# A mixture-of-experts stage: the matrix engine's branch for crowded experts inside the first expert's first piece, and two row gathers ahead of the share arithmetic

## The chip, the cores and the metric

The kernel runs on one core of a Trainium2 chip. The metric is the device time of one execution in microseconds (us): the median of several runs. Engines are named as in the profile: PE is the matrix engine (PEld its weight loads, PEldq its sequencer), DVE the vector engine, ACT the scalar engine, SP the engine that issues the weight transfers (SPq its queue), POOL the general one. A name with a q is the engine's sequencer, which reads the program and hands instructions on.

## The reference, cut to what matters

Two blocks run over the same 256 tokens with 1024 features. The first block has two layers; the second layer ends with a mixture of eight experts, and the change lies there:

```
def moe_swiglu(h, w_router, w_gate, w_up, w_down):
    logits = (xf @ w_router)
    top_logits, top_idx = lax.top_k(logits, TOP_K)          # 2 of 8 experts for a token
    gates = jax.nn.softmax(top_logits, axis=-1)             # the two shares
    ...                                                     # tokens sorted by expert, in blocks of 128
    def expert_block(args):
        xb = xf[tok]
        hb = jax.nn.silu(xb @ w_gate[e]) * (xb @ w_up[e])   # 1024 x 3584 each
        return hb @ w_down[e]                               # 3584 x 1024
    y = yb.reshape(n_rows, D).astype(jnp.float32) * row_gate[:, None]
    out = jnp.zeros((T, D), jnp.float32).at[row_tok].add(y)
```

An expert takes its tokens in blocks of 128. 512 assignments spread over 8 experts, so an expert mostly has fewer than 128; whether one has more is known only when the router has run.

## The kernel before, in words

All products are taken in float32 accuracy from rounded parts: a weight tile is split by ACT into a rounded part (`low_whi`, a CAST) and by DVE into its rest (`low_wlo`, a TENSOR_TENSOR), each in two halves of 128x1024, and PE takes three matmuls of 128x512 for a k-tile of weights: rounded by rounded, rest by rounded, rounded by rest. Weights come in units of 1 MB that SP loads into a ring of buffers as DVE's rests set them free. Each engine's program is written out by hand in one order, and engines meet only at semaphores: `e.wait_ge(*at(...))` waits for the mark that another engine's `then_inc(*mark(...))` sets.

Around the change the work is this. The last projection of the recurrent layer ends (units rg.o.0 to rg.o.3). PE turns the rows and takes the router's logits; DVE picks the two experts of each token, counts, and writes the one-hot selections (`moe_S`). `pe_gather_first` multiplies the normed rows (`moe_hh` and their rest `moe_hl`) by the selections of experts 0 and 1: 32 matmuls of 128x256, into banks 0 to 3, in four parts. ACT scales each part and rounds it (`act_gather`, two ACTIVATEs of 128x256, output `low_hTh`), DVE takes the rest of each part (`dve_gather`, two SCALAR_TENSOR_TENSORs, output `low_hTl`). Then the experts start, as 56 steps (8 experts by 7 pieces of 512 hidden features, `STEPS`); a step has a gate piece (`pe_gate_up` with "g", 24 matmuls into bank 4), an up piece ("u", 24 into bank 5), and from the second step on the down piece of the step before (24). Part q//2 of the gathered rows (mark "xl") is needed by k-tile q of the first gate piece.

Between the gather and the first piece stands `where_over`: each of PE, ACT, DVE and SP loads the largest count of tokens of an expert from memory (TENSOR_LOAD, line 1893), checks it and jumps (COMPARE_BRANCH, line 1894). If the count is over 128, a body follows that computes the tokens beyond the 128th of each expert by plain float32 matmuls; if it isn't, as with these inputs, the engine jumps over the body. PE's body is long: 1872 matmuls. ACT's has 56 ACTIVATEs, DVE's some 300 instructions, SP's 1344 transfers. The body uses banks of the accumulators for its sums.

DVE's order there (`dve_route`): selections, count, the rests of the normed rows, the rests of the unit e0.g0.1 (`lo_after(e, "rg.o.2")`), the share arithmetic (six small operations on `moe_sm`, from `share_e` to `mark("share", 1)`), the four parts of `dve_gather`, the rests of e0.u0.0 (`lo_after(e, "rg.o.3")`), then its own branch.

Of the kernel before, what the change touches and what calls it, by code (L numbers as in the profile page):

```python
# [8 lines left out]
F_DENSE, F_SECOND, F_EXPERT, EXPERTS = 3584, 2816, 3584, 8  # L9
# [33 lines left out]
class Signals:  # L43
# [27 lines left out]
    def at(self, name, *key):  # L71

        if not self.walked and (name, key) not in self.value:
            return self.sem(name), 1
        other, n = self.value[name, key]
        return self.sem(other), n
# [101 lines left out]
def two_block_kernel(nc, A, out):  # L178
    dt, ALU, AX = mybir.dt, mybir.AluOpType, mybir.AxisListType
    AF = mybir.ActivationFunctionType  # L180
# [7 lines left out]
    with ctx:  # L188
        sg = Signals(lambda name: ctx.enter_context(nc.semaphore(name)))
        mark, at, now, also = sg.mark, sg.at, sg.now, sg.also  # L190
# [232 lines left out]
        def lo_after(e, name, half=1):  # L423
            lo_to(e, next_of(name), half)
# [1281 lines left out]
        def dve_route(e):  # L1706
            dve_residual(e, 3, 0, 0)
            dve_residual(e, 3, 0, 1)
            dve_rstd(e, 0)
            dve_hl(e, 0, 0)  # L1710
            dve_hl(e, 0, 1)
            dve_residual(e, 3, 1, 0)
            dve_residual(e, 3, 1, 1)
            dve_rstd(e, 1)

            e.wait_ge(*at("router", "all"))
            e.wait_ge(*at("sum", "logits"))
            e.tensor_copy(mL, AB[0][:, 0:16].rearrange("p (t e) -> p t e", t=2)).then_inc(*mark("logits", "all"))
            e.wait_ge(*at("logits", "all"))
            for tb in range(2):  # L1720
                e.max(mtop[:, tb, :], mL[:, tb, :]).then_inc(*mark("step"))
            e.wait_ge(*now("step"))
            for y in range(2):
                e.tensor_tensor(meq[:, y], mL, by8(mtop[:, :, y]), EQ).then_inc(*mark("step"))
            e.tensor_tensor(mnth[:, 1, :], mtop[:, :, 0], mtop[:, :, 1], EQ).then_inc(*mark("step"))
            e.wait_ge(*now("step"))
            e.tensor_tensor_scan(mcs.rearrange("p k t e -> p (k t e)"), d0[:, :, :, :].rearrange("p k t e -> p (k t e)"),
                                 meq.rearrange("p k t e -> p (k t e)"), 0.0, MUL, ADD).then_inc(*mark("step"))
            e.tensor_scalar(mnth[:, 1, :], mnth[:, 1, :], 1.0, None, ADD).then_inc(*mark("step"))
            e.wait_ge(*now("step"))  # L1730
            for y in range(2):
                e.tensor_tensor(mmask[:, y], mcs[:, y], by8(mnth[:, y]), EQ).then_inc(*mark("step"))
            e.wait_ge(*now("step"))
            e.tensor_tensor(mmask, mmask, meq, MUL).then_inc(*mark("step"))
            e.wait_ge(*now("step"))
            e.tensor_tensor(Mb[:, :, :], mmask[:, 0], mmask[:, 1], ADD).then_inc(*mark("chosen", "all"))
            e.tensor_tensor(mM, mmask[:, 0], mmask[:, 1], ADD).then_inc(*mark("step"))
            e.tensor_tensor(mdiff, mtop[:, :, 1], mtop[:, :, 0], SUB).then_inc(*mark("step"))
            e.wait_ge(*at("rstd", 1))
            e.wait_ge(*now("step"))  # L1740
            e.tensor_tensor(mdiff, rs[:, 1, :, 0], mdiff, MUL).then_inc(*mark("share", 0))
            e.wait_ge(*at("sum", "ranks"))
            e.tensor_copy(posc[:, :], AB[1][:, 0:24]).then_inc(*mark("ranks", "all"))
            also("places", ("all",), "ranks")
            e.wait_ge(*now("step"))
            e.wait_ge(*at("ranks", "all"))
            e.tensor_reduce(mmax, posc[:, 16:24], AX.X, MAX).then_inc(*mark("step"))
            dve_hot(e, 0)
            dve_hot(e, 1)
            e.wait_ge(*now("step"))  # L1750
            e.tensor_copy(cnt[:, :], mmax).then_inc(*mark("count", "all"))
            dve_hl(e, 1, 0)
            dve_hl(e, 1, 1)
            lo_after(e, "rg.o.2")
            e.wait_ge(*at("share_e", "all"))
            e.tensor_scalar(msum, mexp, 1.0, None, ADD).then_inc(*mark("step"))
            e.wait_ge(*now("step"))
            e.reciprocal(mrec, msum).then_inc(*mark("step"))
            e.wait_ge(*now("step"))
            e.tensor_tensor(mg2, mexp, mrec, MUL).then_inc(*mark("step"))  # L1760
            e.tensor_tensor(mt8, mmask[:, 0], by8(mrec), MUL).then_inc(*mark("step"))
            e.wait_ge(*now("step"))
            e.tensor_tensor(mG, mmask[:, 1], by8(mg2), MUL).then_inc(*mark("step"))
            e.wait_ge(*now("step"))
            e.tensor_tensor(mG, mG, mt8, ADD).then_inc(*mark("share", 1))
            for q in range(4):
                dve_gather(e, 0, q)
            lo_after(e, "rg.o.3")


# [39 lines left out]
        def pe_overflow(e):  # L1810
            e.wait_ge(*at("xl", 0, 3))
            for x_ in range(EXPERTS):
                e.wait_ge(*at("ov_hot", x_))
                for tb in range(2):
                    t = e.transpose(bank[7][:, 128 * tb:128 * tb + 128], ov_S[:, tb, :], ident)
                for q in range(KT):
                    for z in range(4):
                        t = e.matmul(bank[q // 4][:, 128 * (q % 4):128 * (q % 4) + 128],
                                     (hh, hl)[z % 2][:, z // 2, 128 * q:128 * q + 128].bitcast(F32), ov_S[:, z // 2, :],
                                     start=z == 0, stop=z == 3)  # L1820
                t.then_inc(*mark("ov_gathered", x_))
                for f in range(7):
                    e.wait_ge(*at("ov_x" if f == 0 else "ov_h", *((x_,) if f == 0 else (x_, f - 1))))
                    for kind, b in (("g", 4), ("u", 5)):
                        for q in range(KT):
                            pe_ov(e, bank[b][:, :], ov_x[:, q, :], (x_, f, kind, q, 0), q == 0, q == KT - 1)
                    e.wait_ge(*at("ov_h", x_, f))
                    for q in range(4):
                        t = e.transpose(bank[6][:, 128 * q:128 * q + 128], ov_h[:, 128 * q:128 * q + 128], ident)
                    t.then_inc(*mark("ov_turned", x_, f))  # L1830
                    e.wait_ge(*at("ov_hT", x_, f))
                    for q in range(4):
                        for n in range(2):
                            pe_ov(e, bank[2 + n][:, :], ov_hT[:, q, :], (x_, f, "d", q, n), (f, q) == (0, 0),
                                  (f, q) == (6, 3))
                e.wait_ge(*at("ov_y", x_))
                for tb in range(2):
                    for n in range(2):
                        t = e.matmul(bank[2 * tb + n][:, :], ov_ST[:, 128 * tb:128 * tb + 128],
                                     ov_y[:, 512 * n:512 * n + 512], start=True, stop=True)  # L1840
                t.then_inc(*mark("ov_scattered", x_))

        def act_overflow(e):
            for x_ in range(EXPERTS):
                for f in range(7):
                    e.wait_ge(*at("ov_used", x_, f, "g", 7, 0))
                    if (x_, f) != (0, 0):
                        e.wait_ge(*at("ov_h", *((x_, f - 1) if f else (x_ - 1, 6))))
                    e.activation(ov_g[:, :], bank[4][:, :], AF.Silu).then_inc(*mark("ov_g", x_, f))

        def dve_overflow(e):
            e.wait_ge(*at("places", "all"))
# [3 lines left out]
            for x_ in range(EXPERTS):  # L1856
# [10 lines left out]
                for f in range(7):  # L1867
                    e.wait_ge(*at("ov_used", x_, f, "u", 7, 0))
                    e.wait_ge(*at("ov_g", x_, f))
                    e.tensor_tensor(ov_h[:, :], ov_g[:, :], bank[5][:, :], MUL).then_inc(*mark("ov_h", x_, f))  # L1870
                    e.wait_ge(*at("ov_turned", x_, f))
                    e.tensor_copy(ov_hT[:, :, :], bank[6][:, :].rearrange("p (k s) -> p k s", k=4)).then_inc(
                        *mark("ov_hT", x_, f))
# [94 lines left out]

        def pe_moe(e):
            pe_route(e)  # L1970
            where_over(e, pe_overflow)
            for c_, (x_, f) in enumerate(STEPS):
                for q in pe_gate_up(e, c_, "g", 0, "msilu"):
                    if c_ == 1 and q == 2:
# [7 lines left out]
                    if x_ % 2 and x_ < EXPERTS - 1 and 2 <= f < 6 and q == 4:  # L1982
                        pe_gather(e, x_ // 2 + 1, f - 2)
                for q in pe_gate_up(e, c_, "u", 1, "mprod"):
                    if x_ and f == 1 and q in (2, 6):
                        pe_scatter(e, x_ - 1, 1, q // 4)
                if c_:
# [1405 lines left out]
```

## Time and profile before

| what | value |
|---|---|
| median of 3 runs | 2329.86 us (2329.62 to 2329.93) |
| the profiled execution | 2329.88 us, its span 2328.1 us |
| PE matmul busy | 2306.1 us (99%), 11387 matmuls |
| DVE busy | 1796.3 us (77%) |
| ACT busy | 1436.0 us (62%) |
| mean granted clock of PE | 0.998 |

The span is the time from the first to the last instruction; some 1.8 us of the execution lie around it. Times in the rows are from the span's start. Matmuls overlap, so that a matmul of 128x512 is shown as 0.39 us while the next starts 0.23 us after it: the pace is read from the starts.

### The profile page before, as it was taken

The page shows a single profiled execution, that of the slowest core. Times are in us where ns is not written, and L with a number is a line of the kernel's source. Part 1 is how long each engine was busy: PE and PEld are TensorE (multiplying, and loading weights), DVE is VectorE, ACT ScalarE, POOL GpSimd, SP SyncE. Part 2 cuts the span into 40 slices and gives each one's busy share as a digit, 9 for nine tenths or more (in the row PEclk, how much of TensorE's full clock was granted, in tenths as well). Part 3 has the DMA queues.
Part 4 walks back from the last instruction along what each step waited for, and adds up shares of the span by engine and source line. Part 5 has one row for each costly group of instructions (what it writes and reads, how often), then busy time and mean ns, then how long its engine had stood idle before and what let it go on. Part 6 is the DMA issues. An engine that isn't in the chain of part 4 may idle for free.

```text
span 2328.1 us, 28882 instructions
## 1 busy us (share of the span) xinstructions
PE 2306.1 (99%) x11387; PEld 1910.2 (82%) x11387; DVE 1796.3 (77%) x2399; ACT 1436.0 (62%) x1985; POOL 7.8 (0%) x17
## 2 busy tenths in 40 slices
PE   9999999899999999999999999999999999999998
PEld 8888889788888888888888888788888877888887
DVE  7755558899999999999899999876754587767554
ACT  6444447677777777777777777554454464555443
POOL 0000000000000000000000000000000000000000
PEclk9999999999999999999999999999999999999999
DMA  8355555599999999999999997545555564555651
GB/s 287 126 197 184 181 181 181 205 343 365 357 358 356 382 349 359 354 380 355 358 361 368 366 353 238 196 144 191 166 195 184 182 209 130 185 185 175 195 182 54
DMA packets 266222, 588.93 MB, mean 253 GB/s; under 512 B 9441, under 2 KB 37361, under 8 KB 265825
## 3 DMA queue, kind: packets, MB, share of 16 engines
q1 hardware_dynamic: 265072, 581.82, 71.4%
q0 software_dynamic: 1008, 5.21, 0.7%
q8 instruction: 91, 1.49, 0.3%
q14 instruction: 51, 0.41, 0.1%
HBM read 585.92 MB, written 1.07 MB: 252 GB/s over the span
## 4 chain that ended last, share of the span: by engine, by line
PE 90%; DVE 8%; ACT 2%; issue 1%; DMA 0%; SPq 0%; DVEq 0%; ACTq 0%
PE ps L106 86%; PE ps L109 4%; DVE low_wlo L121 4%; ACT low_whi L115 1%; DVE s_rot L121 0%; DVE low_nv L127 0%; DVE s_t L121 0%; ACT s_p L112 0%; DVE s_sm L133 0%; DVE ffn_h L121 0%; ACT L112 0%; DMA low_raw<-in_hy_w_in 0%; DVE low_hTl L127 0%; DVE rg_qs L130 0%; ACT low_junk L112 0%
## 5 line engine op out<-in xcount | busy, mean ns | idle before, releaser
L121 DVE TENSOR_TENSOR low_wlo<-low_raw,low_whi 128x1024 fp32r<-128x1024 f32 (+1 forms) x992 | 1158.0, 1212 | 355.7 <-ACT low_whi L115 354.8
L115 ACT CAST low_whi<-low_raw 128x1024 fp32r<-128x1024 f32 (+1 forms) x992 | 984.8, 1043 | 434.9 <-PE ps L106 432.2
L106 PE MATMUL ps<-low_whi,low_hTh 128*128 128x512 f32 (+2 forms) x1616 | 630.1, 393 | 5.3 <-DVE low_wlo L121 3.2
L106 PE MATMUL ps<-low_whi,low_hTl 128*128 128x512 f32 (+2 forms) x1616 | 615.7, 384 | 0.0
L106 PE MATMUL ps<-low_wlo,low_hTh 128*128 128x512 f32 (+2 forms) x1584 | 606.1, 383 | 0.0
L106 PEld LDWEIGHTS ps<-low_whi,low_hTh 128*128 128x128 f32 x1616 | 304.5, 188 | 61.3 <-DVE low_hTl L127 3.6
L106 PEld LDWEIGHTS ps<-low_whi,low_hTl 128*128 128x128 f32 x1616 | 304.1, 188 | 60.3
L106 PEld LDWEIGHTS ps<-low_wlo,low_hTh 128*128 128x128 f32 x1584 | 298.7, 189 | 52.8 <-issue 0.5
L106 PE MATMUL ps<-low_whi,ffn_Th 128*128 128x512 f32 x608 | 243.4, 400 | 0.0
L106 PE MATMUL ps<-low_wlo,ffn_Th 128*128 128x512 f32 x608 | 237.2, 390 | 0.0
L106 PE MATMUL ps<-low_whi,ffn_Tl 128*128 128x512 f32 x608 | 194.3, 390 | 0.0
L106 PE MATMUL ps<-low_whi,moe_xh 128*128 128x512 f32 x448 | 174.7, 390 | 0.0
L106 PE MATMUL ps<-low_whi,moe_xl 128*128 128x512 f32 x448 | 174.3, 389 | 0.0
L106 PE MATMUL ps<-low_wlo,moe_xh 128*128 128x512 f32 x448 | 174.3, 389 | 0.0
L106 PEld LDWEIGHTS ps<-low_whi,ffn_Tl 128*128 128x128 f32 x608 | 114.1, 188 | 25.0
L106 PEld LDWEIGHTS ps<-low_wlo,ffn_Th 128*128 128x128 f32 x608 | 114.4, 188 | 21.8
L106 PEld LDWEIGHTS ps<-low_whi,ffn_Th 128*128 128x128 f32 x608 | 114.3, 188 | 21.7
L121 DVE TENSOR_TENSOR low_wlo<-raw,low_whi 128x1024 fp32r<-128x1024 f32 x102 | 120.1, 1221 | 7.5 <-ACT low_whi L115 7.5
L115 ACT CAST low_whi<-raw 128x1024 fp32r<-128x1024 f32 x102 | 102.0, 1050 | 20.1 <-PE ps L106 20.1
L106 PEld LDWEIGHTS ps<-low_whi,moe_xl 128*128 128x128 f32 x448 | 84.1, 188 | 17.5
L106 PEld LDWEIGHTS ps<-low_whi,moe_xh 128*128 128x128 f32 x448 | 84.1, 188 | 17.2
L106 PEld LDWEIGHTS ps<-low_wlo,moe_xh 128*128 128x128 f32 x448 | 84.1, 188 | 17.2
(359 smaller groups left out, 2315.3 us busy)
## 6 DMA issues: line engine op xcount, KB each, us to landing
low_raw<-in_moe_w_down SPq DMA_DIRECT2D x96, 1024.0 KB, 6.7
low_raw<-in_moe_w_gate SPq DMA_DIRECT2D x95, 1024.0 KB, 6.8
low_raw<-in_moe_w_up SPq DMA_DIRECT2D x94, 1024.0 KB, 6.5
low_raw<-in_w_ffn SPq DMA_DIRECT2D x66, 1024.0 KB, 5.0
low_raw<-in_w_in SPq DMA_DIRECT2D x28, 1024.0 KB, 6.2
low_raw<-in_w_merge SPq DMA_DIRECT2D x24, 1024.0 KB, 5.2
raw<-in_moe_w_up SPq DMA_DIRECT2D x18, 1024.0 KB, 6.8
raw<-in_moe_w_gate SPq DMA_DIRECT2D x17, 1024.0 KB, 6.8
```

What stands on the lines that cost most here:

```text
L106: return self.real.matmul(*a, **k) if self.real else WALK
L109: return self.real.transpose(*a) if self.real else WALK
L115: return self.real.copy(*a) if self.real else WALK
L121: return self.real.tensor_tensor(*a) if self.real else WALK
```

## The change

PE's branch is called inside the first step's up piece, before k-tile 4 of it, in place of ahead of the first gate piece; the other engines' branches stay where they are. Since bank 4 then holds the gate sums and bank 5 the half-made up sums, the body's gate and up sums go to banks 0 and 1, and ACT waits at its body's end until PE has done the body's last scatter. On DVE, parts 0 and 1 of the gathered rows' rests stand ahead of the share arithmetic, parts 2 and 3 behind it.

```diff
@@ dve_route
             lo_after(e, "rg.o.2")
+            dve_gather(e, 0, 0)
+            dve_gather(e, 0, 1)
             e.wait_ge(*at("share_e", "all"))
             e.tensor_scalar(msum, mexp, 1.0, None, ADD).then_inc(*mark("step"))
...
             e.tensor_tensor(mG, mG, mt8, ADD).then_inc(*mark("share", 1))
-            for q in range(4):
-                dve_gather(e, 0, q)
+            dve_gather(e, 0, 2)
+            dve_gather(e, 0, 3)
             lo_after(e, "rg.o.3")
@@ pe_overflow
-                    for kind, b in (("g", 4), ("u", 5)):
+                    for kind, b in (("g", 0), ("u", 1)):
@@ act_overflow
-                    e.activation(ov_g[:, :], bank[4][:, :], AF.Silu).then_inc(*mark("ov_g", x_, f))
+                    e.activation(ov_g[:, :], bank[0][:, :], AF.Silu).then_inc(*mark("ov_g", x_, f))
+            e.wait_ge(*at("ov_scattered", EXPERTS - 1))
@@ dve_overflow
-                    e.tensor_tensor(ov_h[:, :], ov_g[:, :], bank[5][:, :], MUL).then_inc(*mark("ov_h", x_, f))
+                    e.tensor_tensor(ov_h[:, :], ov_g[:, :], bank[1][:, :], MUL).then_inc(*mark("ov_h", x_, f))
@@ pe_moe
             pe_route(e)
-            where_over(e, pe_overflow)
             for c_, (x_, f) in enumerate(STEPS):
...
                 for q in pe_gate_up(e, c_, "u", 1, "mprod"):
+                    if (c_, q) == (0, 4):
+                        where_over(e, pe_overflow)
```

On PE, before, the branch follows the last gather matmul directly (`moe_S`, `moe_hl` are its operands, `moe_cnt` the count):

```order
L106 MATMUL ps<-moe_S,moe_hh 128x256
L106 MATMUL ps<-moe_S,moe_hl 128x256
L1893 TENSOR_LOAD moe_cnt
L1893 ISA x2
L1894 COMPARE_AND_BRANCH
```

and now it stands behind the sixth matmul pair of k-tiles 2 and 3 of the first up piece, whose weights are unit e0.u0.0 (`low_whi_56` rounded, `low_wlo_59` rest):

```order
L106 MATMUL ps<-low_wlo_59,low_hTh 128x512
L106 MATMUL ps<-low_whi_56,low_hTl 128x512
L106 MATMUL ps<-low_whi_56,low_hTh 128x512
L106 MATMUL ps<-low_wlo_59,low_hTh 128x512
L106 MATMUL ps<-low_whi_56,low_hTl 128x512
L1896 TENSOR_LOAD moe_cnt
L1896 ISA x2
L1897 COMPARE_AND_BRANCH
```

36 matmuls moved ahead of the branch: 24 of the gate piece, 12 of the up piece.

On DVE, at the end of the routing, before (`low_hTl` are the rests of the gathered rows, `moe_sm` the share arithmetic, `low_wlo_58` the rests of e0.g0.1, `low_wlo_59` those of e0.u0.0):

```order
L121 TENSOR_TENSOR low_wlo_58<-low_raw_53,low_whi_55 128x1024 x2
L124 TENSOR_SCALAR moe_sm<-moe_sm 128x2
L136 RECIPROCAL moe_sm<-moe_sm 128x2
L121 TENSOR_TENSOR moe_sm<-moe_sm 128x2
L121 TENSOR_TENSOR moe_sm<-moe_sm 128x16 x3
L127 SCALAR_TENSOR_TENSOR low_hTl<-ps,low_col,low_hTh 128x256 x8
L121 TENSOR_TENSOR low_wlo_59<-raw_84,low_whi_56 128x1024 x2
```

and now:

```order
L121 TENSOR_TENSOR low_wlo_58<-low_raw_53,low_whi_55 128x1024 x2
L127 SCALAR_TENSOR_TENSOR low_hTl<-ps,low_col,low_hTh 128x256 x4
L124 TENSOR_SCALAR moe_sm<-moe_sm 128x2
L136 RECIPROCAL moe_sm<-moe_sm 128x2
L121 TENSOR_TENSOR moe_sm<-moe_sm 128x2
L121 TENSOR_TENSOR moe_sm<-moe_sm 128x16 x3
L127 SCALAR_TENSOR_TENSOR low_hTl<-ps,low_col,low_hTh 128x256 x4
L121 TENSOR_TENSOR low_wlo_59<-raw_84,low_whi_56 128x1024 x2
```

Four of the eight operations moved ahead of the six small ones; nothing was added or taken away.

## Rows read from the trace of the kernel before

**Rows 1.** The page: PE's busy line, and the chain that ended last.
```profile
PE 2306.1 (99%) x11387; PEld 1910.2 (82%) x11387; DVE 1796.3 (77%) x2399; ACT 1436.0 (62%) x1985; POOL 7.8 (0%) x17
...
PE 90%; DVE 8%; ACT 2%; issue 1%; DMA 0%; SPq 0%; DVEq 0%; ACTq 0%
```

**Rows 2.** Waits of PE, 440 to 1360 us: total, times, longest.
```profile
PE ps L106 <- DVE low_hTl L127: 2.1, 1, 2.1
PE ps L109 <- DVE ffn_h L121: 0.3, 1, 0.3
```

**Rows 3.** A stretch of experts: length, then PE, PEld, DVE, ACT, POOL, clock, DMA.
```profile
500.00:700.00 200.00, 199.77 (x919) 165.36 (x918) 182.65 (x177) 153.11 (x173) 0.00 (x0) 1.00 0.97 353
```

**Rows 4.** PE in order of time: start, duration, operation, idle before it.
```profile
442.40 0.28 PE L106 MATMUL ps<-moe_S,moe_hl 128*128 128x256 f32 x1
444.73 0.47 PE L106 MATMUL ps<-low_whi,low_hTh 128*128 128x512 f32 x1 [2.05 <-DVE low_hTl L127]
...
451.89 0.39 PE L106 MATMUL ps<-low_whi,low_hTh 128*128 128x512 f32 x1
...
454.61 0.39 PE L106 MATMUL ps<-low_whi,low_hTh 128*128 128x512 f32 x1
```

**Rows 5.** Lines 1893 and 1894: durations in ns, then the start in us.
```profile
L1893 PEldq TENSOR_LOAD <-moe_cnt x1: 490/490/490, 440.4 to 440.4; - x1
...
L1894 PEldq COMPARE_BRANCH  x1: 3320/3320/3320, 441.2 to 441.2; - x1
L1894 ACTq COMPARE_BRANCH  x1: 45/45/45, 443.5 to 443.5; - x1
L1894 DVEq COMPARE_BRANCH  x1: 72/72/72, 445.3 to 445.3; - x1
L1894 SPq COMPARE_BRANCH  x1: 55/55/55, 449.9 to 449.9; - x1
```

**Rows 6.** The chain of waits, 443 to 445 us: start, duration, what.
```profile
443.17 0.80 DVE low_hTl L127 x2
443.97 0.76 issue
```

**Rows 7.** DVE in order of time.
```profile
439.84 2.35 DVE L121 TENSOR_TENSOR low_wlo<-low_raw,low_whi 128x1024 fp32r<-128x1024 f32 x2
442.11 0.17 DVE L124 TENSOR_SCALAR moe_sm<-moe_sm 128x2 f32<-128x2 f32 x1
...
443.09 0.87 DVE L127 SCALAR_TENSOR_TENSOR low_hTl<-ps,low_col,low_hTh 128x256 fp32r<-128x256 f32 x2
...
446.23 2.35 DVE L121 TENSOR_TENSOR low_wlo<-raw,low_whi 128x1024 fp32r<-128x1024 f32 x2
450.47 2.36 DVE L121 TENSOR_TENSOR low_wlo<-raw,low_whi 128x1024 fp32r<-128x1024 f32 x2 [1.89 <-ACT low_whi L115]
```

**Rows 8.** ACT in order of time: parts 0 and 1 of the gathered rows.
```profile
441.28 0.84 ACT L112 ACTIVATE low_hTh<-ps,low_col 128x256 fp32r<-128x256 f32 x2 [1.30 <-PE ps L106]
...
442.00 0.84 ACT L112 ACTIVATE low_hTh<-ps,low_col 128x256 fp32r<-128x256 f32 x2
```

**Rows 9.** Instruction transfers: 442.1 to 443.2, 446.4 to 447.7, 457.3 to 458.4 us.
```profile
q8 instruction: 1, 0.02, 5.2%
...
q8 instruction: 1, 0.02, 5.0%
...
q8 instruction: 1, 0.02, 5.3%
```

**Rows 10.** SP's transfers, 449 to 456 us.
```profile
454.80 0.39 SPq L145 DMA_DIRECT2D raw<-in_moe_w_up  x1
```

**Rows 11.** PE after the pause at 414 us; two stretches with the clock ahead of the last two columns.
```profile
416.28 0.50 PE L106 MATMUL ps<-low_whi,rg_yh 128*128 128x512 f32 x1 [2.16 <-DVE low_wlo L121]
...
415.00:419.00 4.00, 2.34 (x9) 1.61 (x9) 3.94 (x17) 3.88 (x5) 0.00 (x0) 1.00 1.05 394
...
445.70:449.10 3.40, 3.40 (x9) 2.65 (x8) 2.87 (x4) 0.12 (x1) 0.00 (x0) 0.50 0.32 117
```

## The prediction, made before the changed kernel ran

> **What bounds the kernel now.** I read the page first: PE is busy for 99% of the span and makes up 90% of the chain that ended last [rows 1]. So the time moves only by what moves PE's own row of matmuls, and I looked for every place in the expert stage where PE stands. The waits of PE from the gather to the end of the experts are two: 2.1 us once, put down to DVE's gathered rows, and 0.3 us once [rows 2]. In a 200 us stretch of experts PE is busy for 199.77, at full clock, DVE for 182.65 and ACT for 153.11 [rows 3]: PE sets the pace there, and a microsecond that PE starts earlier is a microsecond that it ends earlier. That holds to the end only as PE's work is a chain; nothing in the second block runs by a clock of its own.
>
> Then PE in order of time [rows 4]. The last gather matmul starts at 442.40, the first gate matmul at 444.73: 2.05 us idle. From 451.89 to 454.61 twelve matmuls of 128x512 start, 0.227 us apart. From 444.73 to 454.61 there are 36 of them (24 of the gate piece, 12 of the up piece); at that pace they would take 8.16 us, and they took 9.88, so 1.72 us were lost. The reason stands in [rows 11]: from 445.7 to 449.1 the granted clock was 0.50, the lower of its two levels (1.2 GHz). It fell about a microsecond after the pause. So the place holds two losses: the pause and, behind it, the slow clock.
>
> The profile names DVE as the cause of the pause. The chain says more [rows 6]: DVE's part 0 ends at 443.97, and then 0.76 us pass as "issue" before PE moves. [rows 5] say what they are: PE's sequencer loads the count at 440.4, starts its COMPARE_BRANCH at 441.2, and that takes 3320 ns, so it ends at 444.56, 0.17 us before the first gate matmul. On ACT, DVE and SP the same line takes 45 to 72 ns. PE's rows were late at 443.97, but the branch was later. During it the queue that brings instructions moved a block [rows 9]: PE's body is so long that the place it jumps to had to be brought. SP, with a body of 1344 transfers, shows a short branch at 449.9, yet its next transfer is issued at 454.80 [rows 10], while the rests that free its buffer (those of e0.u0.1) ended at 450.47 + 2.36 = 452.83 [rows 7]: there too about 2 us are gone behind a long jump.
>
> The Trainium skill, "Runtime: NRT & Kernel Launch", section Instruction fetch mechanics, states that a taken branch to code outside the fetched window forces a fetch of the target's page before execution goes on. By that rule the cost travels with the branch, and the trace agrees (3320 ns and one block moved). The skill's "Advanced Engine Details and Errata", section Control Flow Timing, puts a compare-and-branch at about 108 ns; taken by itself that would make the moved branch free, which is the first rival below.
>
> **The change, part by part.**
>
> Start of the gate piece. Two things held it: the branch (444.56) and part 0 of the rests (443.97). The branch is gone from here. On DVE the rests of e0.g0.1 end at 439.84 + 2.35 = 442.19 [rows 7]; ACT's part 0 is done at 441.28 + 0.84 = 442.12 [rows 8], so DVE starts part 0 at about 442.18, and its two operations take 0.87 [rows 7]: 443.05. PE follows in about 0.08, at 443.13. Gain against 444.73: 1.60 us. Part 1 (ACT 442.84, [rows 8]) is done at about 443.85, and k-tile 2 wants it at 443.13 + 6 x 0.227 = 444.49. Then the share arithmetic, 443.09 - 442.11 = 0.98 us [rows 7], stands between; part 2 ends at about 443.85 + 0.98 + 0.79 = 445.6, and k-tile 4 wants it at 443.13 + 2.72 = 445.85; part 3 at 446.4 against 447.2. Part 2 is the tight one, with 0.2 us. The DVE total is unchanged, so the rests of e0.u0.0 end at 448.6 to 448.7 as they do now (446.23 + 2.35 = 448.58), and the first k-tiles of the up piece, due at 443.13 + 24 x 0.227 = 448.58, find their first half long done (447.4).
>
> The slow clock. The pause ahead of the gate piece shrinks from 2.05 us to about 443.13 - 442.68 = 0.45 us. That is less than a quarter of the one behind which the clock fell, and close to the 0.3 us of [rows 2], behind which no pace was lost. I take the 1.72 us as given back.
>
> The new place of the branch. PE's sequencer must have passed the wait of k-tile 2 of the up piece before it gets to the count: that is the end of e0.u0.0's rests, 448.6 to 448.7. It hands on twelve matmuls and loads the count at about 448.85 (0.2 us later; in the trace 0.46 us passed between the last wait ahead of it, DVE's `moe_hl`, and the load, so 0.1 to 0.5 is the range). From load to first matmul it took 444.73 - 440.4 = 4.33 us [rows 4, 5]. So the next matmul starts at about 453.2. Meanwhile PE has what was handed on: 36 matmuls from 443.13 last until 443.13 + 8.16 = 451.29. New pause: 453.2 - 451.29 = 1.91 us. The branch is hidden behind twelve matmuls (2.7 us) and no more, since the rests of e0.u0.0 come only as the up piece starts. Bounds: 0, if the jump costs on PE what it shows on the other engines; 2.3 with the late load and a block that comes 0.1 slower beside weight transfers. I take 1.91, nearest to the one PE row.
>
> Behind it: queued behind the branch are PE's k-tiles 4 to 7, whose rests (e0.u0.1) end by 452.83 even without any shift [rows 7], and everything of PE after. ACT waits for PE's release of the weight buffers and shifts with it; SP and POOL are passed by no moved instruction. The other banks, the changed operands and ACT's added wait lie in bodies that are jumped over: nothing. In exchange the share is made 1.65 us later, and it is needed only at the first scatter in the second expert.
>
> Sum at the 37th matmul: before it starts at 454.61, after at 453.2: -1.60 - 1.72 + 1.91 = -1.41 us. On the profiled execution's 2329.88 (0.02 above the median) that gives 2328.47, say 2328.5 us.
>
> **The rivals.**
>
> The moved branch costs PE nothing, for a short or prefetched jump. For it: 45 to 72 ns on three engines [rows 5]. Against: SP's late transfer, and PE's own row. Then PE goes on at 451.3: -3.3 us, 2326.6.
>
> The clock falls again, in or behind the new pause. This is the one on the other side. In the trace, a pause of 2.05 us was followed by the lower level for 3.4 us, while one of 2.16 us, just ahead of 416.28, was not (415 to 419 shows 1.00, [rows 11]). The new one of 1.9 us is a little shorter than either, but of their kind; before it PE has run 36 matmuls without a stop, where before the fall it had run the smaller matmuls of the gather. If it falls, 1.72 us come back: -1.41 + 1.72 = +0.31, 2330.2, slower than before. It decides from a pause of about 2 us on.
>
> A second block of instructions is late. Behind the branch as it was, the next block moved between 446.4 and 447.7 the second of [rows 9], that is 1.9 to 3.1 us after the branch ended; with the 1.4 us that lay between the first block's transfer and the branch's end, it may be there only 4.5 us after the branch. The new landing place is 36 matmuls further on in the same code, so that much nearer to the block's end. If fewer than some 20 matmuls (4.5 us) stand between, PE pauses once more, by up to 3.1 us with six left; the middle is 1.6: +0.2, 2330.1, and at worst 2331.6. For it: after 444.7 the third block moved only between 457.3 and 458.4 the third of [rows 9], when PE was 48 matmuls past the old landing; if that marks the block's end, it lies 50 or more matmuls behind it, so some 14 to 25 behind the new one. That is at the edge; I think it mostly covered.
>
> The gain is eaten later, by DVE or ACT, and the time stays at 2329.9. Against: rows 2, no wait of PE on a weight rest in the whole stage.
>
> **How the numbers follow.** Forecast 0.52, free branch 0.12, the clock falls again 0.18, second block late 0.12, eaten 0.06. All of them lie between -3.3 and +1.8 us. 0.2% is 4.7 us, about what a measurement of this kernel can tell from no change; the pause and the slow clock together are 3.8 us, so even their whole loss would not reach it. Faster by over 0.2%: 0.02. Slower: 0.03, for two of the rivals at once with a worse size. Within: 0.95. The range goes from the free branch to the second block with 0.2 us of the measurement: 2326.5 to 2330.5. The likeliest case's own range is 2328.0 to 2328.9.
>
> **What would show it.** First gate matmul at 443.1 to 443.2, with some 0.4 us idle before it; full clock from 442 to 451; PE's TENSOR_LOAD at about 448.9 and a COMPARE_BRANCH of about 3.3 us; a pause of 1.7 to 2.1 us inside the up piece, ended by no other engine, its next matmul near 453.2; no lower clock behind it; the same distance of 1.4 us at the end of the experts. It is wrong if PE's branch is short, if the sequencer loads the count well before the up piece starts, if the clock falls, or if part 2 of the rests comes after k-tile 4 is due.

## The result, and the profile after

The change costs 4.6 us. Over 16 runs of each kernel on the same chip the median is 2334.52 us after (2332.03 to 2336.56) against 2329.89 before (2327.64 to 2331.37): a ratio of 1.0019 [1.0012, 1.0026], slower, though by just under the 0.2% that counted as a change in the forecast. The forecast was 2328.5 us, and all 16 runs lie above its range. The execution with the profile took 2333.81 us, its span 2332.0 us, 3.9 us more than before. In these 16 runs the mean granted clock goes with the time: 0.998 in the one of 2332.03 us, 0.995 in the one of 2336.56 us.

The page first: PE's busy line and the chain, which answer to [rows 1], and the group of matmuls with most idle time before it.

```profile
PE 2308.6 (99%) x11387; PEld 1912.2 (82%) x11387; DVE 1795.8 (77%) x2399; ACT 1436.2 (62%) x1985; POOL 7.8 (0%) x17
...
PE 90%; DVE 7%; ACT 2%; issue 1%; DMA 0%; SPq 0%; DVEq 0%; ACTq 0%
...
L106 PE MATMUL ps<-low_whi,low_hTh 128*128 128x512 f32 (+2 forms) x1616 | 630.8, 393 | 7.6 <-issue 4.1
```

PE has as many matmuls and is busy 2.5 us longer, for which the clock further down is the only cause that the rows show; and one group now shows 4.1 us of idle time that no engine ended. The waits of PE from the gather to the end of the experts (total, times, longest) say the same against [rows 2]: the pause of 2.1 us on DVE is 0.4 us, the one of 0.3 us is gone, and one of 4.1 us is new.

```profile
PE ps L106 <- issue: 4.1, 1, 4.1
PE ps L106 <- DVE low_hTl L127: 0.4, 1, 0.4
```

PE in order of time after the change (start, duration, operation, idle before it), to be laid beside [rows 4]:

```profile
442.69 0.28 PE L106 MATMUL ps<-moe_S,moe_hl 128*128 128x256 f32 x1
443.38 0.50 PE L106 MATMUL ps<-low_whi,low_hTh 128*128 128x512 f32 x1 [0.41 <-DVE low_hTl L127]
...
451.44 0.39 PE L106 MATMUL ps<-low_whi,low_hTl 128*128 128x512 f32 x1
455.96 0.79 PE L106 MATMUL ps<-low_whi,low_hTh 128*128 128x512 f32 x1 [4.13 <-issue]
456.55 0.63 PE L106 MATMUL ps<-low_wlo,low_hTh 128*128 128x512 f32 x1
456.98 0.63 PE L106 MATMUL ps<-low_whi,low_hTl 128*128 128x512 f32 x1
...
462.94 0.60 PE L109 MATMUL ps<-low_cst,ffn_h 128*128 128x128 f32 x4
```

The gate piece starts 1.35 us earlier (443.38 against 444.73), although the gather itself ended 0.29 us later in this execution. 36 matmuls run at 0.23 us apart; then PE stands for 4.13 us, and the matmuls behind are 0.43 us apart. The 37th matmul starts at 455.96, 1.35 us later than before; the transposes of `ffn_h`, which come 18 matmuls later (twelve that end the up piece and six of the next gate piece), start at 462.94, where before they did at 458.70: 4.24 us later. Nearly all of that is kept to the end (3.9 us).

The count's load and the branch in the changed kernel (durations in ns, then the start in us; [rows 5] of before):

```profile
L1896 PEldq TENSOR_LOAD <-moe_cnt x1: 485/485/485, 449.0 to 449.0; - x1
...
L1897 ACTq COMPARE_BRANCH  x1: 45/45/45, 443.8 to 443.8; - x1
L1897 DVEq COMPARE_BRANCH  x1: 72/72/72, 445.8 to 445.8; - x1
L1897 PEldq COMPARE_BRANCH  x1: 6068/6068/6068, 449.8 to 449.8; - x1
L1897 SPq COMPARE_BRANCH  x1: 55/55/55, 450.2 to 450.2; - x1
```

PE's branch jumps over a body of the same instructions, for the same count, and takes 6.07 us where it took 3.32. The next rows say what is different around it: SP's transfers, then the packets of three windows by queue (count, MB, share of the engines), from the branch's start to 453.4, from there to 454.5, and around 460. The last row is of the kernel before, the first 0.9 us of its branch (441.2 to 442.1).

```profile
448.94 0.37 SPq L145 DMA_DIRECT2D raw<-in_moe_w_gate  x1
455.06 0.94 SPq L145 DMA_DIRECT2D raw<-in_moe_w_up  x2
```

```profile
q1 hardware_dynamic: 513, 1.03, 90.8%
q14 instruction: 2, 0.02, 1.6%
...
q8 instruction: 1, 0.02, 5.8%
q1 hardware_dynamic: 15, 0.01, 3.8%
...
q1 hardware_dynamic: 240, 0.46, 100.8%
q8 instruction: 1, 0.02, 5.2%
```

```profile
DMA packets 0, 0.00 MB, mean 0 GB/s; under 512 B 0, under 2 KB 0, under 8 KB 0
```

SP issues 1 MB of weights 0.9 us before PE's branch. While these packets run, no block of PE's instructions moves. It starts at 453.45, as the weights run dry, 3.62 us after the branch began; before the change it started 0.94 us after (442.18 against 441.24), when no weight transfer was under way: SP's was issued at 442.22. The rest is as it was: 1.03 us for the block (0.91 before), 1.42 us from there to the branch's end (1.47 before).

The clock ahead of the last two columns, in three stretches (length, PE, PEld, DVE, ACT, POOL, clock, DMA): the 36 matmuls, the stretch of low clock behind the pause, and one ahead of the place of the change.

```profile
443.30:451.80 8.50, 8.43 (x36) 6.68 (x36) 7.99 (x18) 7.28 (x11) 0.00 (x0) 1.00 0.58 176
434.60:438.00 3.40, 3.40 (x21) 3.33 (x20) 2.47 (x20) 3.37 (x6) 0.00 (x0) 0.50 0.01 2
...
455.10:461.90 6.80, 5.94 (x14) 4.68 (x15) 0.42 (x1) 0.36 (x1) 0.00 (x0) 0.50 0.84 297
```

The lower level (1.2 GHz) begins in the pause, 0.9 us before PE goes on, and lasts 6.8 us, twice as long as in [rows 11]. The 18 matmuls from there to the transposes took 462.94 - 455.96 = 6.98 us, where before it took 458.70 - 454.61 = 4.09: 2.89 us for the clock.

Last DVE, whose rests the share arithmetic now interrupts:

```profile
444.41 0.66 DVE L121 TENSOR_TENSOR moe_sm<-moe_sm 128x2 f32<-128x2 f32 x4
445.00 1.65 DVE L127 SCALAR_TENSOR_TENSOR low_hTl<-ps,low_col,low_hTh 128x256 fp32r<-128x256 f32 x4
446.57 2.35 DVE L121 TENSOR_TENSOR low_wlo<-raw,low_whi 128x1024 fp32r<-128x1024 f32 x2
449.29 4.63 DVE L121 TENSOR_TENSOR low_wlo<-raw,low_whi 128x1024 fp32r<-128x1024 f32 x4 [0.38 <-issue]
461.48 0.69 DVE L121 TENSOR_TENSOR ffn_h<-ffn_g,ps 128x512 f32<-128x512 f32 x1 [7.56 <-PE ps L106]
```

The rests of e0.u0.0 end at 446.57 + 2.35 = 448.92, PE loads the count at once (448.98), and later DVE waits 7.56 us for PE: DVE holds nothing up.

### The profile page after: what moved, and what is told of

It reads as the page before. It is cut to its first block, busy times and chain, and to the rows that moved or that the text cites. A ratio compares the mean times of both kernels' runs of the same rounds, so it can differ in the third digit from the quotient of the medians.

```text
span 2332.0 us, 28882 instructions
## 1 busy us (share of the span) xinstructions
PE 2308.6 (99%) x11387; PEld 1912.2 (82%) x11387; DVE 1795.8 (77%) x2399; ACT 1436.2 (62%) x1985; POOL 7.8 (0%) x17
## 4 chain that ended last, share of the span: by engine, by line
PE 90%; DVE 7%; ACT 2%; issue 1%; DMA 0%; SPq 0%; DVEq 0%; ACTq 0%
PE ps L106 86%; PE ps L109 4%; DVE low_wlo L121 3%; DVE s_rot L121 0%; ACT low_whi L115 0%; DMA low_raw<-in_hy_w_in 0%; DVE s_t L121 0%; DVE low_hTl L127 0%; ACT s_p L112 0%; DVE s_sm L133 0%; DVE low_nv L127 0%; ACT L112 0%; DVE rg_qs L130 0%; DVE ffn_h L121 0%; ACT ffn_g L112 0%
## 5 line engine op out<-in xcount | busy, mean ns | idle before, releaser
L115 ACT CAST low_whi<-low_raw 128x1024 fp32r<-128x1024 f32 (+1 forms) x992 | 984.9, 1043 | 442.2 <-PE ps L106 439.3
```

Source lines behind the costliest of these rows:

```text
L115: return self.real.copy(*a) if self.real else WALK
```

## The experiments

Theory A, formed on these rows: the block of code at the branch's target waits for the transfers that are already on their way, so the branch costs 3.3 us in a quiet spot and more beside a weight transfer; the lower clock comes with the long pause. Against it stood: a branch that is dearer at this place whatever the transfers do (B, the landing place); and DVE's new order, which may hold PE up (C). "Fetch" below is the start of the 16 KB block on queue 8 after the branch's start, as the packets of the trace have it. Before, in the three sessions: 2331.05, 2329.98 and 2329.87 us (medians of 33, 27 and 15 runs). The ratios with their 95% intervals are those on record; they are not the quotients of these medians, and some differ from them by up to 0.06%.

**No weight transfer under way.** SP takes its own branch one transfer earlier, and then holds that transfer until PE is past the up piece.

```diff
-            sync_weights(e, 4, routed)
+            sync_weights(e, 4, routed - 1)
             where_over(e, sync_overflow)
-            sync_weights(e, routed, len(units))
+            e.wait_ge(*at("sum", "u", 0))
+            sync_weights(e, routed - 1, len(units))
```

> The changed kernel, with SP's branch one transfer earlier and the one weight transfer of 1 MB that was in flight during PE's branch (issued at 448.9 us) held until PE has made the first up sums. In the changed kernel PE's COMPARE_BRANCH took 6.07 us in place of the 3.32 us at its old place; its block of code began to move only 3.6 us after the branch began, as that transfer ended, and before it was 0.9 us. Theory A, the block waits behind the weight transfer: the branch takes 3.2 to 3.6 us here, the pause shrinks from 4.1 to about 1.5 us, and the time falls by 2.7 us and by what the clock gives back, to 2328.5 to 2331. Theory B, the landing place in the code or the crossing of a block just before the branch makes it long: 6 us, pause 4 us, time within 1 us of the changed kernel's 2334.5.

PE's branch, then PE behind it, then the packets from 452.2 to 453.5 and from there to 454.6:

```profile
L1897 PEldq COMPARE_BRANCH  x1: 3708/3708/3708, 452.2 to 452.2; - x1
```

```profile
455.94 0.50 PE L106 MATMUL ps<-low_whi,low_hTh 128*128 128x512 f32 x1 [1.76 <-DVE low_wlo L121]
```

```profile
DMA packets 0, 0.00 MB, mean 0 GB/s; under 512 B 0, under 2 KB 0, under 8 KB 0
...
q8 instruction: 1, 0.02, 5.3%
```

The fetch comes 1.36 us after the branch, alone on the engines; the branch takes 3.71 us, a little more than the 3.6 expected, the pause is 1.76 us (1.91 was forecast for the change), and no lower clock follows. 2329.76 us, a ratio to before of 0.9998 [0.9989, 1.0007]. The slowdown is gone with the transfer. A gain isn't shown, and the interval doesn't exclude the 1.4 us of the forecast.

**Half the weight transfer.** After, with 512 KB of the 1 MB issued ahead of SP's branch and the rest held.

```diff
-            sync_weights(e, 4, routed)
+            sync_weights(e, 4, routed - 1)
...
+            load(e, "half", u.raw[:, 0:2, :], u.src[:, 0:2, :])
             where_over(e, sync_overflow)
+            e.wait_ge(*at("sum", "u", 0))
+            e.wait_ge(*at("d_half", "in"))
+            e.dma_start(u.raw[:, 2:4, :], u.src[:, 2:4, :]).then_inc(sg.sem(f"raw{u.slot.i}"), 16)
```

> The changed kernel with only the first half (512 KB) of the weight transfer issued at 448.9 us; the second half is held until PE has made the first up sums. The block of PE's code began to move 3.6 us after the branch began beside the whole transfer (1 MB) and 1.4 us after it with none in flight. Theory A, the block waits until the transfer in flight is through: the start comes in between, 2 to 2.8 us after the branch began, and the branch takes 4.3 to 5.1 us. Rival, any transfer in flight costs the same (a slot in a queue, not the bytes ahead): 3.3 us or more to the start, branch 5.7 us or more.

PE's branch, and the packets of its first 2.4 us:

```profile
L1897 PEldq COMPARE_BRANCH  x1: 4808/4808/4808, 449.2 to 449.2; - x1
```

```profile
q1 hardware_dynamic: 271, 0.52, 76.5%
q14 instruction: 1, 0.01, 0.8%
```

Fetch 2.43 us after the branch, pause 2.87 us, one execution at 2331.03 us. Between no transfer (3.71 us) and 1 MB (6.07), as A has it. SP's own branch is one more thing beside PE's: in the changed kernel it comes 0.4 us after it (450.21). Here it comes just as near (449.55 against 449.18) and PE's is 1.3 us shorter, so it isn't SP's jump that makes the difference.

**The same cost put into the kernel before.** Before, with 768 KB more of weights issued by SP just ahead of PE's branch. They go to a tile that nothing reads; ACT and DVE wait for them behind their own branches (two lines that the diff leaves out).

```diff
-            sync_weights(e, 4, routed)
+            sync_weights(e, 4, routed - 2)
+            e.wait_ge(*at("hl", 1, 1))
+            load(e, "extra", extra[:, :, :], rows_of(A["moe_w_gate"][0, 0], 0, 384, 0, 512))
+            sync_weights(e, routed - 2, routed)
```

> The kernel before, in its old order, with one more transfer of 768 KB by SP (weights into a region that is free then; nobody reads them), issued when DVE has the last rests of the normed rows, at about 440.0 us, a microsecond ahead of PE's branch at 441.2. Theory A: the block of PE's code starts only as that transfer ends, 2.5 to 4 us after the branch began in place of 0.9, the branch takes 5 to 6.5 us in place of 3.3, the first gate matmul comes at 446.5 to 448 and the time rises by 2 to 3 us. Theory B (landing place): the branch stays at 3.3 us and the time at that of before within 0.5 us.

The transfer and the branch, and PE behind it:

```profile
439.50 0.37 SPq L145 DMA_DIRECT2D ov_extra<-in_moe_w_gate  x1
```

```profile
L1895 PEldq COMPARE_BRANCH  x1: 5200/5200/5200, 440.8 to 440.8; - x1
```

```profile
446.16 0.77 PE L106 MATMUL ps<-low_whi,low_hTh 128*128 128x512 f32 x1 [3.93 <-DVE low_hTl L127]
```

With the branch at its old place and the old order of PE's and DVE's work, the transfer alone makes it 5.20 us (fetch after 2.73), the pause 3.93 us and the clock low for 6.8 us, from 0.8 us before PE goes on. The first gate matmul comes at 446.16, just before the 446.5 to 448 expected. 2332.53 us, 1.0013 [1.0004, 1.0022]. That speaks against B and C. The packets of the 1.1 us from the block's start also show what it waits for:

```profile
q1 hardware_dynamic: 147, 0.29, 86.6%
q8 instruction: 1, 0.02, 5.4%
```

Another 0.29 MB of weights moved beside it; SP had issued its next transfer at 441.77, after the branch. It looks as if only what was ahead of the block had to pass first. The kernels with a short body below agree: SP issues another 1 MB 1.4 us after PE's branch began (452.99 with three pieces), and the fetch starts 3.5 to 3.7 us after the branch, as in the changed kernel (3.62).

**No branch.** After, with PE's branch and body left out.

```diff
-                        where_over(e, pe_overflow)
+                        if e.real is None:
+                            pe_overflow(e)
```

> The changed kernel without PE's branch and its body (left out: PE's part of the work for experts with over 128 tokens, which these inputs never need); the other engines keep theirs. If the branch is the whole cause (theories A and B alike), there is no pause in the first up piece, no lower clock behind it, and the time is 4.1 us of pause and 2 to 3.4 us of slow clock below the changed kernel's 2334.5, that is 2326.5 to 2328.5: 1.5 to 3.5 below the kernel before. If something else in the change slows it (the order on DVE, the second block of code), the time stays above 2330.

No pause stands in its place, and the transposes start at 456.06 (458.70 before). 2327.93 us, 0.9993 [0.9984, 1.0002]. The whole branch is worth 1.6 us by this ratio (0.0007 x 2330), which the interval can't tell from nothing; its other end is 3.7 us, so how much the best place could bring stays open.

**One half of the change at a time.** First only PE's branch moved, with DVE's old order; then only DVE's new order, in the kernel before.

```diff
-            dve_gather(e, 0, 0)
-            dve_gather(e, 0, 1)
             e.wait_ge(*at("share_e", "all"))
...
-            dve_gather(e, 0, 2)
-            dve_gather(e, 0, 3)
+            for q in range(4):
+                dve_gather(e, 0, q)
```

> Only PE's branch is moved, with its banks; DVE's order is that of before. The gate piece then starts when part 0 of the rests is there, at about 444.0 (after 0.98 us of share arithmetic) in place of 443.1 to 443.4, and everything up to the branch's load hangs on DVE's rests of e0.u0.0, which do not move. So the branch lies at the same time, 6 us long under theory A and B, the pause before it is 1 us longer and the one at the branch 1 us shorter: the same time as the changed kernel within 1 us, 2333.5 to 2335.5. If the DVE order mattered by itself, it would differ by more.

```profile
PE ps L106 <- issue: 2.9, 1, 2.9
PE ps L106 <- DVE low_hTl L127: 1.3, 1, 1.3
PE ps L109 <- DVE ffn_h L121: 0.3, 1, 0.3
```

The waits of PE with the branch alone moved: 1.3 us for the gathered rows instead of 0.4, so DVE's order does bring its 0.9 us there, and 2.9 us at the branch, which takes 5.74 us (fetch after 3.32). 2332.08 us, 1.0010 [1.0001, 1.0019]. The new place of the branch is enough for a slowdown, though one at the edge of what these runs can tell. It was expected at 2333.5 to 2335.5 and came out below. Both halves together reach the 37th matmul no sooner (13.27 us after the last gather matmul, 13.00 here), since the end of PE's branch hangs on DVE's rests of e0.u0.0; what DVE's new order adds is a longer pause there, 4.1 us in place of 2.9, and this profile shows no lower clock with the shorter one. The runs fit that: the mean granted clock is 0.998 in seven of the 11 here, and in three of the 16 of the changed kernel.

```diff
+            dve_gather(e, 0, 0)
+            dve_gather(e, 0, 1)
             e.wait_ge(*at("share_e", "all"))
...
-            for q in range(4):
-                dve_gather(e, 0, q)
+            dve_gather(e, 0, 2)
+            dve_gather(e, 0, 3)
```

> The kernel before with the new order on DVE alone. PE's branch ends at 444.5 whatever DVE does, so the gate piece starts at 444.7 as before: 2329.9 within 0.5 us, and the branch 3.3 us long. If the rests of the gathered rows had held PE (as the profile's releaser says), the start would come 0.7 to 1.5 us earlier.

DVE's order alone: pause 2.09 us instead of 2.05, branch 3.36 us, 2329.8 us, 1.0000 [0.9991, 1.0009]. The branch ended last there, so earlier rows bring nothing. The profiled execution shows no lower clock behind this pause and took 2327.60 us, the fastest of its 11; one came behind the same pause in [rows 11], in an execution of 2329.88. The medians are the same: which execution shows it is not fixed by the kernel.

**A shorter body, so a shorter jump.** After, with a body of one expert; then with one expert and 1, 3 or 5 of its 7 pieces. The jump passes 234, 66, 122 and 178 matmuls instead of all experts' (some 476, 134, 248 and 362 instructions of PE, an estimate from the code with a weight load for each matmul).

```diff
-        ov_all = [p for x_ in range(EXPERTS) for p in ov_pieces(x_)]
+        ov_all = [p for x_ in range(1) for p in ov_pieces(x_)]
...
-            for f in range(7):
+            for f in range(1):
                 for kind, w in (("g", A["moe_w_gate"]), ("u", A["moe_w_up"])):
```

> The changed kernel with a short body on all four engines: only the first expert's part (234 matmuls on PE in place of 1872; the parts of experts 1 to 7 are left out, which these inputs never run). Place of the branch, transfers in flight and matmul order are those of the changed kernel. Theory A (the branch is long because the place it jumps to is not in the engine's instruction memory, and the block that must come waits behind a weight transfer): with the target near enough, the branch takes under 0.2 us, no pause, and the time is that of the kernel without the branch, 2326.5 to 2329. Rival: reading the count, the check and the jump have their own price on PE: the branch stays at several us and the time near 2334.5. If the length that the memory holds is below 234 matmuls, the branch stays at 3 to 6 us too; the next kernel tells that apart.

6.03 us, fetch after 3.57, pause 4.08 us, 2333.05 us, 1.0014 [1.0005, 1.0024]: as long as over the whole body, where A expected under 0.2 us, or 3 to 6 if one expert's body is still too long.

> As the last, with one expert and one of its seven pieces in the body (66 matmuls on PE; the rest left out, never run by these inputs). Theory A: PE's COMPARE_BRANCH under 0.2 us, whatever the last one showed. Rival: 3 to 6 us.

PE's branch and the waits of PE, with one piece:

```profile
L1897 PEldq COMPARE_BRANCH  x1: 365/365/365, 450.9 to 450.9; - x1
```

```profile
PE ps L109 <- DVE ffn_h L121: 0.7, 2, 0.4
PE ps L106 <- DVE low_hTl L127: 0.4, 1, 0.4
```

0.37 us (under 0.2 was expected) and no pause at the branch; one execution at 2328.14 us.

> The changed kernel with one expert and three of its seven pieces in the body (122 matmuls on PE, some 250 instructions with their weight loads; the rest left out, never run by these inputs). 66 matmuls gave a branch of 0.37 us, 234 one of 6.0. Theory A only asks for a length at which it changes; by one block of some 256 instructions ahead of the engine, 122 matmuls lie at the edge, 0.1 to 3.5 us; if what is held ahead is longer, 0.4 us or less.

> As the last, with five of seven pieces (178 matmuls, some 360 instructions). If the length that decides lies between 122 and 178 matmuls: 5.5 to 6.5 us; if it lies above: 0.4 us or less.

The branch with three pieces, and PE behind it:

```profile
L1897 PEldq COMPARE_BRANCH  x1: 454/454/454, 451.6 to 451.6; - x1
```

```profile
457.62 0.59 PE L106 MATMUL ps<-low_whi,low_hTh 128*128 128x512 f32 x1 [4.02 <-issue]
```

Five pieces: 6.17 us and a pause of 4.23 us, 2336.44 us in one execution. Three pieces are the surprise: the branch row is as short as with one piece, and PE stands 4.02 us all the same (2335.2 us in one execution). The block is fetched at 455.11, behind the weights. So here the wait is not in the row of the branch, but in front of the instructions behind it. The price begins between 134 and 248 instructions and, from there to the whole body, stays at a pause of 4.0 to 4.2 us.

**Trying for a better version.** The kernel with the held transfer, and the share arithmetic behind all four parts and the rests of e0.u0.0, so that the count is read earlier in the up piece.

```diff
             dve_gather(e, 0, 1)
+            dve_gather(e, 0, 2)
+            dve_gather(e, 0, 3)
+            lo_after(e, "rg.o.3")
             e.wait_ge(*at("share_e", "all"))
```

> The changed kernel with the held transfer, and on DVE the share arithmetic (0.98 us) behind the rests of e0.u0.0, so that PE's sequencer gets past its last wait and to the count a microsecond earlier. Theory A, with 3.7 us for the branch as with the held transfer alone: load of the count 0.9 to 1.0 us earlier against the first gate matmul (4.6 to 4.8 us behind it in place of 5.6), pause 0.7 to 1.1 us in place of 1.76, time 0.9 us below the held transfer's 2329.8, that is 2328.9, and 1 to 2 us below before. Rival: the queue holds no more than some 12 matmuls, and the pause stays at 1.7 us.

DVE from 450 us on:

```profile
450.53 0.66 DVE L121 TENSOR_TENSOR moe_sm<-moe_sm 128x2 f32<-128x2 f32 x4
455.08 4.63 DVE L121 TENSOR_TENSOR low_wlo<-raw,low_whi 128x1024 fp32r<-128x1024 f32 x4 [3.89 <-issue]
```

PE loads the count 4.63 us after its first gate matmul (5.61 with the transfer held alone), and its branch ends at 454.57. But DVE's own branch now stands right ahead of the rests of e0.u0.1. Its row shows 72 ns at 451.9, and DVE stands 3.89 us; PE goes on only at 456.36, put down to DVE: a pause of 2.21 us where 0.7 to 1.1 was expected. 2331.68 us, 1.0006 [0.9997, 1.0015], and not the 2328.9 hoped for.

The last one keeps that order and places the branches of ACT and DVE behind their work on e0.u0.1.

```diff
             act_route(e)
-            where_over(e, act_overflow)
             e.activation(msm[:, 222:223], num[:, 5:6], AF.Silu)
+            hi_after(e, "e0.g0.0")
+            where_over(e, act_overflow)
...
             dve_route(e)
+            lo_after(e, "e0.g0.0")
             where_over(e, dve_overflow)
```

> The changed kernel with the held transfer, the share arithmetic behind the rests of e0.u0.0, and, so that DVE's own jump is not exposed (with the share last it stood for 3.9 us before the rests of e0.u0.1, and PE went on 1.8 us after its branch's end), the branches of ACT and DVE one unit later, behind the rounding and the rests of e0.u0.1. Theory A: count loaded 4.6 us after the first gate matmul, branch 3.4 to 3.8 us, PE goes on 0.1 to 0.3 us after its end, pause 0.6 to 1.1 us, no lower clock behind it; against the held transfer alone (pause 1.76) 0.7 to 1.1 us less: 2328 to 2329, below before by 0.05 to 0.1%, at the edge of what five rounds can tell. Rival, the moved branches of ACT or DVE take their toll in the next step: a new wait of PE on DVE's rests of 1 us or more.

PE around its branch (3.70 us, from 450.13):

```profile
452.68 0.39 PE L106 MATMUL ps<-low_whi,low_hTl 128*128 128x512 f32 x1
453.89 0.50 PE L106 MATMUL ps<-low_whi,low_hTh 128*128 128x512 f32 x1 [0.83 <-issue]
```

The pause is 0.83 us with no lower clock behind it, and the transposes start 13.52 us after the first gate matmul (458.11 - 444.59), where before they did 13.97 us after. 2329.2 us, 0.9996 [0.9987, 1.0005]: the lowest median of those with the whole body, and not to be told from the kernel before.

## Why the prediction was wrong

**Start of the gate piece: right.** 443.13 was forecast; the gather ended 0.29 us later in this execution (442.69 against 442.40), and the piece started at 443.38. Parts 2 and 3 of the rests were in time: nothing stands between the 36 matmuls.

**Load of the count: right.** 448.85 forecast, 448.98 measured.

**The new pause: this step failed.** It was put at 1.91 us with 2.3 as its bound, and it is 4.13. "From load to first matmul it took 4.33 us" was taken from the one PE row and carried to the new place; there it is 455.96 - 448.98 = 6.98. Of the 2.65 us too many, 2.68 lie in the one part fetch (3.62 against 0.94 us). The bound did name "a block that comes 0.1 slower beside weight transfers", but weighed the block's own transfer (1.03 against 0.91 us, right) and not the time until it may start. The rows were there: [rows 10] and the trace around it have SP's transfers at 442.2, 448.6 and 454.8. The old branch began just before one, the new one was forecast for 449.7, right behind one. 1 MB in flight shows it on the changed kernel (6.07 us), 512 KB less (4.81), none least (3.71), and 768 KB at the old place (5.20 against 3.32). That the transfers cause the wait is shown by these; whether the block waits in a queue of each DMA engine or in memory is not.

**The slow clock: half right.** It was counted as given back (1.72 us) behind the shorter first pause, and so it was: 1.00 over the 36 matmuls. But it came back with the new one, for 2.89 us. The second rival had it, with "from a pause of about 2 us on" as the point from which it decides; its price was that of a 2 us pause. In the profiles it fell in or behind every pause of 3.9 us or more at this branch (the change, one expert, three and five pieces, the added transfer), behind three of the five pauses of 2 to 3 us there, and behind none shorter. That a gain of 1.72 us was booked on one execution was a mistake of its own: with DVE's order alone the profiled execution had the pause without the lower clock and was 2.3 us faster than that of [rows 11], while the median was the same. What the median of the kernel before would give back is not known.

**The sum.** At the 37th matmul: -1.35 for the start, -1.72 for the clock, +0.13 for a longer first matmul, and +4.29 from the start that was next due (451.44 + 0.23) to 455.96, together +1.35, where -1.41 was forecast. With 2.89 us of clock that is +4.24 at the transposes. 0.3 us come back, since the old wait of 0.3 us on `ffn_h` is gone from [rows 2].

**The other rivals.** A free branch, for a short jump, is what one piece shows (0.37 us), so its condition was real, but the body is not short. A late second block: the next one moved at 459.49, and PE had no second pause; refuted. A gain eaten later: refuted, since from the transposes to the end of the span it takes 1869.4 us before, 1869.1 after and 1869.4 with the transfer held. With the transfer held, the 37th matmul starts 10.92 us after the last gather matmul in the profile, 1.29 less than the 12.21 before, which had the lower clock, and 0.27 more than the 10.65 of DVE's order alone, which had not. So without the wait for the weights the forecast's -1.41 us nearly comes out, against an execution with the lower clock; why the median shows none of it is open.

The Trainium skill, "Runtime: NRT & Kernel Launch", section Instruction fetch mechanics, says that a taken branch outside the fetched window must fetch its target's page first. The runs agree (0.37 us over 134 instructions, 6.2 over 362).

## What to carry to other kernels

A branch over a long body is a 16 KB load with a queue in front of it: place it where no large transfer was issued in the microseconds before, not only where an engine has work to cover it. When a stall is moved, look at every shared resource at its new place, and not only at the rows that release it. And a stretch of lower clock in one execution is no term of a sum until a second execution shows it.

## What the runs showed of the hardware

- A far taken branch on PE: 3.3 to 3.7 us with nothing ahead of it (0.9 to 1.4 us to the block's start, 0.9 to 1.3 for 16 KB, 1.4 to 1.5 to the end), 4.8 with 512 KB of weights in flight, 5.2 with 768 KB, 5.7 to 6.2 with 1 MB.
- The cost need not stand in the row of the branch: 72 ns and 3.89 us of standing on DVE, 454 ns and 4.02 us on PE. The profile then names "issue", or the engine's last product. SP's row is 55 to 59 ns in all of them; behind the jump over its whole body its next transfer comes 2.0 us (before) and 3.4 us (after) after the rests that free its buffer (454.80 against 452.83, 455.06 against 451.65), with one expert's body at once (452.40 against 452.37).
- All five pauses of PE of about 4 us at this branch came with 3.4 or 6.8 us at the lower clock, which cost up to 2.9 us more. In four of them it began 0.8 to 1.2 us before PE went on, in the fifth (one expert) 0.4 us behind.
- The same kernel's executions differ by up to 4.5 us (2332.03 to 2336.56), and stretches of lower clock of 3.4 or 6.8 us appear near 51, 416 or 435 us in some of the profiles, well ahead of the place that was changed.
